# Sixteen more short products of ones ahead of and between the token sums of a transformer block

## The chip, the cores and the metric

The kernel runs on one core of one Trainium2 chip. The metric is the device time of one execution in microseconds (us), from the launch of the program to its end. Engines are named as in the profile: PE is TensorE (matrix products), PEld its weight loads, DVE is VectorE, ACT is ScalarE, POOL is GpSimd, SP is SyncE, which here issues nearly all DMA transfers.

## The reference

The reference is one layer of a diffusion backbone with 256 latent and 256 context tokens of width 2048, in float32. The parts at the start of the layer are the ones that matter here.

```python
mod_lat = jnp.split((jax.nn.silu(c) @ w_mod[layer] + b_mod[layer])[:, None, :], N_MOD, axis=-1)
mod_ctx = jnp.split(jax.nn.silu(c_ctx) @ w_mod[layer] + b_mod[layer], N_MOD, axis=-1)
...
u_lat = modulate(rms_norm(h_lat, norm_mix_w[layer]), mod_lat[0], mod_lat[1])
u_ctx = modulate(rms_norm(h_ctx, norm_mix_w[layer]), mod_ctx[0], mod_ctx[1])
k_na, v_na, k_ret, v_ret, q_na, q_ret, g_ret = jnp.split(u_lat @ w_in[layer], LAT_SPLITS, axis=-1)
```

After that come two kinds of attention, an output projection, a second norm, a router and 16 experts of three 2048 x 1024 matrices each, whose weights are most of the 593 MB that the kernel moves.

## The kernel before

The program is written out by hand, one instruction stream for each engine, with semaphores between them. SP's stream loads the tokens in four pieces of 1 MB (`xnT`, line 485), and then the weights in items of 1 MB (line 514) in one fixed order into a ring of slots. An item ("mod", i, q) holds part q of 4 of the modulation weights for two 128-wide slices, an item ("w", b, q) part q of 4 of block b of the input projection. Eight groups of modulation items (i = 0 to 7) and the items of blocks 0 and 1 come first. SP waits for a slot to be given back before it loads into it a second time.

PE's stream opens so. The norm of each token needs the sum of its squares. ACT squares piece j (line 1069), DVE folds it (lines 1350 and 1351) and says so with `folded`, and PE adds it over the partitions with four products with a column of ones, `token_sums(j)` (line 735). When all four are in, DVE forms the mean (line 1353), POOL the root (line 1826), DVE four diagonal pieces (line 1357), and PE spreads them over the partitions (line 757). `mod_item(i, q)` (line 592) multiplies an item of modulation weights with the two conditioning vectors, 16 products of 32 x 512. `mod_sums(i)` (line 603) adds them up, `project(b, k)` (lines 636 to 638) multiplies a slice of the normed tokens with a slice of `w_in`. `keep_clock(n)` (line 746) is n products of a 128 x 128 tile of ones with itself. They go to a bank whose content is not used, and they wait for nothing but PE itself. The trace has two matmul records for each float32 product.

In this order PE's stream goes on without a choice at run time:

```python
pe.wait_ge(c_act, 2)
mod_item(0, 0)
mod_item(0, 1)
pe.wait_ge(diag_ok, 1)
mm(bank[4][:, :], ones[:, :], diag, start=True, stop=True).then_inc(rstd_pe, 1)
mod_item(0, 2)
mod_item(0, 3)
keep_clock(2)
mod_sums(0)
keep_clock(10)
pair(0)
for i in range(1, MOD_BEFORE - 1):
    mod_item(i, 0)
```

`pair(0)` is project(0, 0) and project(1, 0). After it come the four items of i = 1, and from there a group of modulation items and two steps of the projection by turns. `mod_item` waits for its item's landing (`wait_item`), and `project` for the split of its weights by ACT (line 1093) and DVE (line 1427).

Of the kernel before, what the change touches and what calls it, by code (L numbers as in the profile page):

```python
# [180 lines left out]
def build(nc, x, x_cols, cond, w_mod_a, w_mod_b, b_row, w_in, rpb, w_out,  # L181
# [301 lines left out]
    def _(sp):  # L483
# [49 lines left out]
        for i in ring_items[:RING]:  # L533
            d = moe_pairs[ring_place(i)]
            if i == 2:
                sp.wait_ge(masks, 8)
                sp.dma_start(extra_a[:, :, :].rearrange("p a n -> p (a n)"), w_down[0, EXTRA - 8][:, 0:2048]).then_inc(extra_full, 16)
                sp.wait_ge(roped, ROPED)
                sp.wait_ge(ret_mix_a, 4)
                sp.wait_ge(a_ready, MOD_BEFORE + 1)  # L540
                sp.dma_start(extra_b[:, :, :].rearrange("p a n -> p (a n)"), w_down[0, EXTRA - 8][:, 2048:3584]).then_inc(extra_full, 16)
            if d < 2:
                for s in (2 * d, 2 * d + 1):
                    _, b0, q0 = items[max(n for n in range(n_items) if slot[n] == s)]
                    sp.wait_ge(lo_split, place(b0, 4 * q0 + 3) + 1)
            if d == 4:
                sp.wait_ge(chunk_used, CHUNKS * (NB + NO))
                sp.dma_start(extra_c[:, :], w_down[0, EXTRA - 8][:, 3584:4096]).then_inc(extra_full, 16)
                for s in range(2):
                    sp.dma_start(halves[s][:, :], w_gate[0, SPLIT][:, 2048 * s:2048 * s + 2048]).then_inc(half_full[s], 16)  # L550
            if d == 5:
                sp.wait_ge(r_pe, 1)
            expert_item(0, i, ring_place(i))
# [28 lines left out]
    def _(pe):  # L582
# [148 lines left out]
        def token_sums(j):  # L731

            pe.wait_ge(folded, j + 1)
            for t in range(4):
                last = mm(bank[5][:, t:t + 1], stat[:, j, P * t:P * t + P], ones[:, 0:1], start=j == t == 0, stop=j == 3 and t == 3)
            last.then_inc(token_sq, 1)
# [6 lines left out]
        def keep_clock(n, b=3):  # L743

            for _ in range(n):
                mm(bank[b][:, 0:P], ones[:, :], ones[:, :], start=True, stop=True)

        pe.wait_ge(pool_init, 2)
        keep_clock(18)
        for j in range(4):  # L750
            token_sums(j)
            keep_clock(5 if j < 3 else 1)
        pe.wait_ge(c_act, 2)
        mod_item(0, 0)
        mod_item(0, 1)
# [1224 lines left out]
```

## Time and profile before

| what | value |
|---|---|
| median of 3 runs | 1686.28 us |
| lowest and highest run | 1685.04, 1690.88 us |
| the profiled execution's own time | 1685.8 us |
| its span, first to last instruction | 1683.7 us |
| mean granted TensorE clock | 0.914 |
| PE busy | 1446.7 us (86%) |
| DMA | 593.05 MB, mean 352 GB/s |

The span leaves out 2.1 us around the instructions. How to read them: the work between the launch and the first instruction and behind the last is in the run's time and not in the span. The page cuts the span into 40 equal slices of 42 us. A clock of 1.0 there is 2.4 GHz, one of 0.5 is 1.2 GHz.

### The profile page before, as it was taken

Reading aid. Unit: us, or ns where it says so; the run is one execution under the profiler, and the core shown is the slowest. Engines: PE = TensorE matmul, PEld = TensorE weight load, DVE = VectorE, ACT = ScalarE, POOL = GpSimd, SP = SyncE. Lnnn points to the kernel's source line nnn. Section 1 sums busy time; section 2 is a strip of 40 time slices with the busy share of each in tenths; the row PEclk is TensorE's granted clock in tenths of the full one; section 3 lists DMA queues with packets and bytes.
Section 4 is the critical chain, followed back from the end, with each engine's and each line's share of the span. In section 5 each row is a group of like instructions: output and inputs, shape, how many; then the busy total and the mean of one; then the engine's idle time right before and its main releaser. Section 6 shows DMA issues by size and latency. Waiting matters only on the chain.

```text
span 1683.7 us, 19822 instructions
## 1 busy us (share of the span) xinstructions
PE 1446.7 (86%) x8024; PEld 862.2 (51%) x8024; DVE 713.8 (42%) x1150; ACT 328.0 (19%) x576; POOL 124.3 (7%) x113
## 2 busy tenths in 40 slices
PE   8999999999999999989878687767787677786786
PEld 6678788878888777875212241321332122332232
DVE  4446777678778876662122122112221211421122
ACT  3343333233333345530000000000000000000001
POOL 0000000013322254001000000000000000000002
PEclk8999999999999999999878798787888978977899
DMA  9996658657746767899999999999999999999996
GB/s 398 420 422 233 227 200 300 226 212 254 257 153 247 274 226 156 214 421 427 428 428 427 426 428 429 428 428 427 422 420 428 429 427 428 427 428 428 428 428 281
DMA packets 55980, 593.05 MB, mean 352 GB/s; under 512 B 6348, under 2 KB 6476, under 8 KB 8152
## 3 DMA queue, kind: packets, MB, share of 16 engines
q1 hardware_dynamic: 54584, 585.66, 86.3%
q10 hardware_dynamic: 1312, 6.16, 1.0%
q8 instruction: 66, 1.08, 0.3%
q14 instruction: 18, 0.15, 0.0%
HBM read 588.65 MB, written 2.10 MB: 351 GB/s over the span
## 4 chain that ended last, share of the span: by engine, by line
PE 52%; DMA 41%; DVE 4%; issue 1%; ACT 1%; SPq 0%; POOL 0%; DVEq 0%; POOLq 0%; ACTq 0%
DMA ring<-in_w_up 18%; DMA ring<-in_w_down 17%; PE bank L640 7%; PE bank L642 7%; PE bank L641 7%; PE bank L993 5%; PE bank L927 3%; PE bank L636 3%; PE bank L637 2%; PE bank L638 2%; PE bank L906 2%; PE bank L592 2%; DMA ring<-in_w_gate 2%; PE bank L894 1%; DMA ring<-in_w_down_last 1%
## 5 line engine op out<-in xcount | busy, mean ns | idle before, releaser
L993 PE MATMUL bank<-ring,xg 128*32 128x512 f32 x1504 | 219.6, 713 | 126.9 <-DMA ring<-in_w_up 96.1
L1427 DVE TENSOR_TENSOR whl<-ring,whl 128x512 fp32r<-128x512 f32 x276 | 211.2, 768 | 133.9 <-ACT whl L1093 132.6
L1093 ACT ACTIVATE whl<-ring 128x512 fp32r<-128x512 f32 x276 | 173.1, 629 | 271.0 <-PE bank L642 212.1
L640 PE MATMUL bank<-whl,uh 128*128 128x512 f32 x512 | 206.5, 403 | 2.0 <-DVE tmp L1456 0.7
L642 PE MATMUL bank<-whl,ul 128*128 128x512 f32 x512 | 199.8, 390 | 0.0
L641 PE MATMUL bank<-whl,uh 128*128 128x512 f32 x512 | 199.5, 390 | 0.0
L993 PEld LDWEIGHTS bank<-ring,xg 128*32 128x32 f32 x1504 | 44.9, 120 | 280.1 <-DMA ring<-in_w_up 148.2
L1410 DVE SCALAR_TENSOR_TENSOR part<-ring,csT,part 128x1024 f32<-128x1024 f32 x104 | 140.0, 1346 | 0.1
L1293 ACT ACTIVATE gup<-bank 128x512 f32<-128x512 f32 x32 | 18.7, 597 | 599.0 <-PE bank L993 599.0
L906 PE MATMUL bank<-yy,gcur 128*128 128x512 f32 x252 | 130.3, 642 | 4.7 <-DVE yy L1714 3.5
L1768 DVE COPY gup<-bank 128x512 f32<-128x512 f32 x32 | 22.0, 689 | 247.5 <-PE bank L993 247.4
L1714 DVE TENSOR_TENSOR yy<-bank,m 128x512 f32<-128x512 f32 x64 | 40.0, 684 | 188.5 <-PE bank L927 185.0
L1721 DVE TENSOR_TENSOR acc<-acc,bank 128x512 f32<-128x512 f32 x96 | 65.8, 687 | 125.8 <-PE bank L906 125.8
L640 PEld LDWEIGHTS bank<-whl,uh 128*128 128x128 f32 x512 | 96.2, 188 | 25.9 <-DVE tmp L1456 2.0
L642 PEld LDWEIGHTS bank<-whl,ul 128*128 128x128 f32 x512 | 96.1, 188 | 20.6
L641 PEld LDWEIGHTS bank<-whl,uh 128*128 128x128 f32 x512 | 96.3, 188 | 19.0 <-issue 0.5
L927 PE MATMUL bank<-ring,hT 128*32 128x512 f32 x480 | 67.3, 690 | 34.1 <-DMA ring<-in_w_down 34.1
L906 PEld LDWEIGHTS bank<-yy,gcur 128*128 128x128 f32 x252 | 44.7, 199 | 98.6 <-issue 79.8
L636 PE MATMUL bank<-uh,whl 128*128 128x512 f32 (+1 forms) x256 | 90.7, 354 | 0.7 <-DVE kT L1438 0.4
L637 PE MATMUL bank<-uh,whl 128*128 128x512 f32 (+1 forms) x256 | 86.3, 337 | 0.0
L638 PE MATMUL bank<-ul,whl 128*128 128x512 f32 (+1 forms) x256 | 86.1, 336 | 0.0
L962 PEld LDWEIGHTS bank<-small,gup 128*128 128x128 f32 x512 | 77.2, 241 | 10.3 <-ACT gup L1293 10.3
(263 smaller groups left out, 1623.1 us busy)
## 6 DMA issues: line engine op xcount, KB each, us to landing
ring<-in_w_up SPq DMA_DIRECT2D x61, 2048.0 KB, 26.0
ring<-in_w_gate SPq DMA_DIRECT2D x33, 2048.0 KB, 25.9
ring<-in_w_mod_b SPq DMA_DIRECT2D x63, 1024.0 KB, 5.3
ring<-in_w_down SPq DMA_DIRECT2D x30, 2048.0 KB, 27.0
ring<-in_w_in SPq DMA_DIRECT2D x53, 1024.0 KB, 5.0
ring_b<-in_w_gate SPq DMA_DIRECT2D x15, 2048.0 KB, 21.6
ring_c<-in_w_gate SPq DMA_DIRECT2D x15, 2048.0 KB, 24.1
ring<-in_w_mod_a SPq DMA_DIRECT2D x28, 1024.0 KB, 16.2
```

The lines of the kernel that those rows point to most:

```text
L636: mm(to, wh[:, cols], hi[:, k, 0:n], start=k == 0 and not (shared and t >= 2), stop=False)
L637: mm(to, wl[:, cols], hi[:, k, 0:n], start=False, stop=False)
L638: last = mm(to, wh[:, cols], lo[:, k, 0:n], start=False, stop=k == KC - 1 and not (shared and t < 2))
L640: mm(ps, hi[:, k, cols], wh, start=k == 0, stop=False)
L641: mm(ps, hi[:, k, cols], wl, start=False, stop=False)
L642: last = mm(ps, lo[:, k, cols], wh, start=False, stop=k == KC - 1)
L906: mm(comb_bank(g, ei, cb, t)[:, :], gcur[:, P * t:P * t + P], yy[:, cb, :], start=True, stop=True).then_inc(comb, 1)
L927: last = mm(bank[cb][32 * quad:32 * quad + 32, :], hT[:, r, :], pieces[4 * (r % 2) + cb], start=r < 4, stop=r >= 4)
L993: last = mm(bank[2 * m + half][32 * kk:32 * kk + 32, :], xg[:, 4 * j + kk, CAP * ei:CAP * ei + CAP], parts[kk // of][0][:, kk % of, 512 * ...
L1093: a(whl[:, cidx % (AHEAD + 1), 0, :], slot_buf(slot[n])[:, 512 * (k % 4):512 * (k % 4) + 512], ACT.Copy).then_inc(hi_split, 1)
L1410: ins = v.scalar_tensor_tensor(out=acc, in0=w, scalar=csT[:, k, 0:1], in1=acc, op0=ALU.mult, op1=ALU.add)
L1427: v.tensor_tensor(whl[:, cidx % (AHEAD + 1), 1, :], slot_buf(slot[n])[:, 512 * (k % 4):512 * (k % 4) + 512], whl[:, cidx % (AHEAD + 1), 0, ...
```

## The change

Only the arguments of five calls of `keep_clock` change. There are 25 calls instead of 18 ahead of the first token sum, 12 instead of 5 behind it, 6 instead of 5 behind the second and the third, and 1 as before behind the fourth. That is 16 calls more, or 32 records of the trace.

```diff
         pe.wait_ge(pool_init, 2)
-        keep_clock(18)
+        keep_clock(25)
         for j in range(4):
             token_sums(j)
-            keep_clock(5 if j < 3 else 1)
+            keep_clock((12, 6, 6, 1)[j])
         pe.wait_ge(c_act, 2)
```

PE's instructions at the start of the program, where `ones` is the tile of ones, `stat` the folded squares and x the number of calls in a row:

```order
-L746 MATMUL bank<-ones 128x128 x18
+L746 MATMUL bank<-ones 128x128 x25
 L735 MATMUL bank<-ones,stat 128x1 x4
-L746 MATMUL bank<-ones 128x128 x5
+L746 MATMUL bank<-ones 128x128 x12
 L735 MATMUL bank<-ones,stat 128x1 x4
-L746 MATMUL bank<-ones 128x128 x5
+L746 MATMUL bank<-ones 128x128 x6
 L735 MATMUL bank<-ones,stat 128x1 x4
-L746 MATMUL bank<-ones 128x128 x5
+L746 MATMUL bank<-ones 128x128 x6
```

No instruction has changed its place. PE's stream is longer by the 16 calls, and those of DVE, ACT, POOL and SP are the same.

## Rows read from the trace of the kernel before

**Rows 1.** Page: PE, the clock and the DMA rows of the 40 slices

```profile
PE   8999999999999999989878687767787677786786
...
PEclk8999999999999999999878798787888978977899
DMA  9996658657746767899999999999999999999996
GB/s 398 420 422 233 227 200 300 226 212 254 257 153 247 274 226 156 214 421 427 428 428 427 426 428 429 428 428 427 422 420 428 429 427 428 427 428 428 428 428 281
```

**Rows 2.** Timeline of PE, 1 to 31 us: start, length, line, operation, count, [idle before]

```profile
1.45 6.32 PE L746 MATMUL bank<-ones 128*128 128x128 f32 x36 [1.45 <-POOL mhalf L1823]
9.64 1.05 PE L735 MATMUL bank<-ones,stat 128*128 128x1 f32 x8 [1.87 <-DVE stat L1351]
10.55 1.36 PE L746 MATMUL bank<-ones 128*128 128x128 f32 x10
13.63 1.87 PE L735 MATMUL bank<-ones,stat 128*128 128x1 f32 x8 [1.71 <-DVE stat L1351]
15.36 2.48 PE L746 MATMUL bank<-ones 128*128 128x128 f32 x10
...
23.74 3.13 PE L592 MATMUL bank<-ring,csT 128*32 128x512 f32 x16
26.81 1.12 PE L757 MATMUL bank<-pb,ones 128*128 128x512 f32 x2
27.86 1.92 PE L592 MATMUL bank<-ring,csT 128*32 128x512 f32 x16
```

**Rows 3.** Busy time by stretch: bounds, length, engines (records), granted clock, DMA, GB/s

```profile
7.77:12.58 4.81, 2.27 (x18) 2.08 (x18) 2.74 (x3) 2.56 (x4) 0.00 (x0) 1.00 1.02 429
12.58:16.00 3.42, 2.37 (x11) 2.38 (x12) 2.82 (x4) 2.84 (x2) 0.00 (x0) 0.50 1.00 424
...
22.82:26.23 3.41, 3.41 (x16) 1.29 (x20) 1.03 (x5) 0.00 (x0) 1.02 (x1) 0.50 1.01 420
26.23:34.23 8.00, 7.56 (x59) 4.44 (x51) 4.21 (x11) 3.13 (x6) 0.00 (x0) 1.00 1.02 423
```

**Rows 4.** Timeline of DVE, 12 to 28 us: the folds, the mean, the diagonal

```profile
12.88 0.69 DVE L1351 TENSOR_TENSOR stat<-sq 128x512 f32<-128x512 f32 x1
...
17.85 0.69 DVE L1351 TENSOR_TENSOR stat<-sq 128x512 f32<-128x512 f32 x1
23.21 0.16 DVE L1353 TENSOR_SCALAR rs<-bank 128x4 f32<-128x4 f32 x1 [4.68 <-PE bank L735]
24.67 0.87 DVE L1357 TENSOR_SCALAR pb<-small,rs 128x128 f32<-128x128 f32 x4 [1.29 <-POOL rs L1826]
```

**Rows 5.** Tile `ring` on SP's queue, 4.45 to 4.90: the transfer of item (mod, 0, 3)

```profile
L514 SPq DMA_DIRECT2D ring<-in_w_mod_a x1: 495/495/495, 4.4 to 4.4; - x1
...
DMA to landing us min/median/max: 21.6/21.6/21.6
```

**Rows 6.** The same, 12.55 to 12.60: item (mod, 1, 3), and who waited

```profile
L514 SPq DMA_DIRECT2D ring<-in_w_mod_a x1: 2107/2107/2107, 12.6 to 12.6; - x1
...
  PEld bank L592: 0.5, 1
...
DMA to landing us min/median/max: 28.4/28.4/28.4
```

**Rows 7.** Weight loads of PE at the items of i = 1

```profile
40.35 0.13 PEld L592 LDWEIGHTS bank<-ring_c,csT 128*32 128x32 f32 x4 [0.30 <-issue]
40.97 0.37 PEld L592 LDWEIGHTS bank<-ring,csT 128*32 128x32 f32 x8 [0.49 <-DMA ring<-in_w_mod_a]
```

**Rows 8.** Timeline of PE, 38.5 to 42.5 us: the products of these items

```profile
41.21 1.04 PE L592 MATMUL bank<-ring,csT 128*32 128x512 f32 x8
42.18 0.50 PE L636 MATMUL bank<-uh,whl 128*128 128x512 f32 x1
```

**Rows 9.** Busy time by stretch, columns as before: the stage of modulation, and late ones

```profile
41.21:60.00 18.79, 18.79 (x126) 13.29 (x119) 6.80 (x19) 6.32 (x12) 0.00 (x0) 1.00 1.01 420
60.00:100.00 40.00, 40.00 (x266) 27.62 (x265) 18.79 (x42) 15.38 (x27) 0.00 (x0) 1.00 1.01 420
100.00:130.00 30.00, 30.00 (x198) 21.59 (x197) 15.46 (x33) 13.92 (x24) 0.00 (x0) 1.00 0.99 403
130.00:160.00 30.00, 30.00 (x145) 25.32 (x144) 20.66 (x27) 12.23 (x20) 0.00 (x0) 1.00 0.60 225
...
674.80:678.10 3.30, 3.30 (x13) 2.73 (x12) 3.19 (x5) 2.46 (x6) 0.00 (x0) 0.50 1.00 417
```

## The prediction

> **What bounds the kernel now.** I read the page first. The slices show two regimes [rows 1]: PE at 9 tenths through the first 17 or so slices, and DMA at 9 tenths in the first three and again from slice 18 to the end, at 420 to 429 GB/s. So the first three slices, where the change lies, are full on both sides, and a gain on PE has to be held against the stream of weights there.
>
> Next I read PE's own timeline at the start [rows 2]. The reader is to see two things. The engine has a gap of 1.87 us ahead of the first token sum and one of 1.71 us ahead of the second, with only 10 records of ones between. And the same group of 10 records takes 1.36 us at 10.55 and 2.48 us at 15.36. The granted clock says why [rows 3]: it falls from 1.00 to 0.50 (2.4 to 1.2 GHz) at 12.58, behind a stretch of 4.81 us in which PE was busy for 2.27, and it comes back at 26.23, after the first modulation products. From 13.63 to 26.23 all PE work is at half speed, and PE has no gap in it.
>
> Then I asked who would have held PE there at full speed. DVE's folds end at 12.88 + 0.69 = 13.57 and 17.85 + 0.69 = 18.54 [rows 4], yet DVE starts the mean of all four only at 23.21, after 4.68 us of idling for PE. So PE is the late one there.
>
> Last I asked what PE meets behind that. Item (mod, 0, 3) lands at 4.4 + 21.6 = 26.0 [rows 5], and item (mod, 1, 3) at 12.6 + 28.4 = 41.0 [rows 6]. For the second of these the weight load of PE already idles 0.49 us and starts at 40.97, where the one before it started at 40.35 [rows 7], so the landing is just ahead of 40.97; the products that need it start at 41.21 [rows 8]. PE is kept from a gap only because 0.24 us of earlier products were still in it. **That is the place which decides.**
>
> **The change part by part.** The ones ahead of the first sum: 14 records more. At full speed one costs 1.36 / 10 = 0.136 us by its group of 10. The first 36 took 6.32 us, 0.176 us each, so a part of them ran slower; the added ones come last. 14 x 0.136 = 1.9 us at most, against a gap of 1.87 us whose end DVE sets [rows 2]. Cost 0 to 0.1 us on a sum that is not late.
>
> Behind the first sum: 14 records more, again up to 1.9 us, against 1.71 us of gap [rows 2]. The 24 records start at 10.55 and end by about 13.3 to 13.8 where DVE's fold is there at 13.57. Cost 0 to 0.2 us.
>
> Behind the second and third: 2 records more each, 0.27 us at full speed, 0.5 us at half speed (2.48 / 10 = 0.25 each).
>
> What they are to bring is the full clock through the opening. At full speed a token sum takes 10.55 - 9.64 = 0.91 us and 12 records of ones 12 x 0.136 = 1.6 us, together 2.5 us, which is DVE's own pace (12.88 to 17.85 is two folds, 2.5 us each). So the last sum starts by DVE's last fold, at 18.6, and ends at about 19.6 where it ended at 23.2: **3.6 us earlier**. Two modulation items (16 records) take 1.92 us at 27.86 [rows 2] in place of 3.13, another 1.2 us, so that PE spreads the diagonal at about 22.0 (mean at 19.6, then the same 24.67 + 0.87 - 23.21 = 2.3 us to the diagonal [rows 4]) in place of 26.81. **Up to here 4.8 us are gained.**
>
> Now the stream takes it back. Item (mod, 0, 3) is the second half of the pair at 27.86, used from 27.86 + 0.9 = 28.8 on, and is not there before 26.0: of the 4.8 us, 2.8 are left. By the same steps as before (mod_sums, the new norms, pair(0)) PE comes to the items of i = 1 about 2.8 us earlier. There (mod, 1, 3) is not in before 40.9, and its products can start no earlier than some 0.05 us behind the load at 40.97. They started at 41.21. **0.2 us are left.** Nothing makes the transfer itself earlier: its issue at 12.6 waits for no use of a slot, as it is a first filling, and up to 130 us DMA is 0.99 to 1.02 busy at 403 to 424 GB/s [rows 3, 9], so its queue is never empty. From 41 us on PE has no gap up to 130 and beyond [rows 9], and 0.2 us passes on. At 130 DMA's share falls to 0.60, and later the experts' stream starts on what PE has done, so the 0.2 us should reach the end.
>
> A page of the Trainium skill bears on that limit. DMA: Bandwidth & Descriptors, section Where 436 GB/s comes from, puts the limit of transfers from HBM at about 358 GB/s for a core and that of the fabric at 435. The trace disagrees with the first (420 to 429 GB/s, one core busy) and agrees with the second. Were the opening held to 358 GB/s instead, item (mod, 1, 3) would land some 7 us later and the change would be worth nothing at all; at 435 it would land about 1.2 us sooner, and about 1.4 us of gain would be left.
>
> Sum against the profiled execution: 1685.8 - 0.2 = 1685.6 us. That execution lies 0.5 us under the median of the runs shown. In other executions the clock may come back later than 2.5 us behind the first modulation product (23.74 to 26.23). A spell of half clock that goes on for another 3.3 us, as the one at 674.80 lasts [rows 9], would hold the kernel before up by half of that, 1.65 us, and the changed kernel not. So the gain against the median lies between 0.2 and 1.9 us, and I take the middle, 0.9: **1685.4 us**, or 0.05%. About 0.3% (5.1 us) is what a measurement of this kernel can tell from no change; the three runs shown are 5.8 us apart.
>
> **The rivals.** *The gain passes.* If item (mod, 1, 3) were not a wall (it lands earlier, or its use can be put off by other work), 2.8 us would remain from the first wall, 1683.0, and with none at all 4.8 us, 1681.0. For it speak the 4.68 us for which DVE plainly idles for PE [rows 4]; against it the 0.49 us of idling of the weight load, which is a direct record.
>
> *Slower: the clock falls at the new wall.* PE gets to the items of i = 1 about 2.8 us early. An item of 1.05 MB at 421 GB/s lands every 2.5 us, so (mod, 1, 2) is in at 38.5, where PE asks for it at 41.21 - 0.96 - 2.8 = 37.5 or so, and (mod, 1, 3) at 40.95, where PE is through with the one before it at 39.4 (an item takes 1.92 / 2 = 0.96 us): gaps of 1.0 and 1.6 us within 5 us. In the opening such a pattern, 2.54 us of idling in 4.81, was followed by the low clock [rows 3]. Here a fall would hit work that bounds the kernel from 41 us on. A spell of 3.3 to 3.5 us [rows 9] costs half of itself, 1.7 us: 1685.8 - 0.2 + 1.7 = 1687.3. It decides the sign from a spell of 0.4 us on, and is seen in a measurement only from 10.2 us on. The spell of the opening, 26.23 - 12.58 = 13.65 us, would cost 6.8 us: 1692.4; but there PE had little to do, and here the projections stand ready. The gaps are also shorter than there and the items between them dense.
> The Trainium skill has this as a rule, in TensorE: Matmul & The Clock Gate, section HAM oscillation — how this bites in real kernels: bursts of products that are cut by waits for transfers start cold again and again. By it this rival would be the likeliest, since the change turns a slow but even PE into a fast one that waits for DMA.
>
> *The change doesn't hold the clock.* 12 records between the second, third and fourth sum are only 2 more than in the group that preceded the fall. If the clock falls anyway, at 12.6 or at 16, the opening is as before or slightly better, the wall is the same, and the time is 1685.6 to 1685.8. At half clock the four added records there cost 1.0 us of PE, of which the wall has 0.2 to hide: at worst 1686.5.
>
> **How the numbers follow.** The wall holds and PE stays fast: 0.70. The clock is not held: 0.10. The gain passes: 0.06. The clock falls at the wall: 0.14, with 0.03 of it for a long spell. Over 0.3% faster needs 1681.2 or less: the 4.8 us case of the first rival, and chance in the runs, 0.05. Over 0.3% slower, 1691.3 or more: the long spell and chance, 0.05. Within: 0.90. The range goes from the case of 2.8 us, 1683.0, to the short spell with 1.2 us on top for the scatter of the runs, 1688.5.
>
> **What the profile should show.** Right: PE's row of ones at 1.45 has 50 records and ends near 9.4, the granted clock is 1.00 to past 30, DVE's L1353 starts near 19.6 in place of 23.21, L757 near 22 in place of 26.81. Then PE idles for DMA ahead of L592, for about 3 us in all before 41, and the products of (mod, 1, 3) start at 41.0. Wrong: they start clearly earlier than 40.9 (the stream isn't the wall), or a stretch behind 36 us has a clock of 0.50 (the rival on the slow side), or L1353 starts near 23 (the clock wasn't held). A difference of over 3 us with these products still at 41.0 would mean that something behind 130 us moved, for which I have no mechanism.

## The result, and the profile after

| kernel | median | runs | lowest, highest |
|---|---|---|---|
| before | 1685.36 us | 22 | 1683.61, 1690.88 |
| changed | 1689.26 us | 22 | 1685.16, 1692.33 |

The ratio is 1.0020, with a 95% interval of 1.0013 to 1.0026. The change makes the kernel 3.9 us slower. The prediction was 1685.4 us, 0.05% faster, with a range that ends at 1688.5. It was wrong in sign and range. The difference is under the 0.3% that the text took for the limit of a measurement, but over 22 runs on each side it stands clear of none. The profiled execution took 1689.32 us, with a span of 1687.5.

The page of the changed kernel, its first line and the DMA rows of the slices that answer to [rows 1]:

```profile
span 1687.5 us, 19886 instructions
...
PEclk9999999999999999999988788887788877977899
DMA  9996658657646757799999999999999999999997
GB/s 396 421 421 233 225 200 302 224 216 254 251 160 241 289 208 169 197 425 427 427 428 428 428 427 427 428 428 428 413 395 427 428 428 428 428 428 428 428 427 294
```

There are 64 instructions more than the 19822 of the kernel before: each of the 16 calls is two weight loads and two products. The first slice's clock is at 9 tenths in place of 8. And slices 28 and 29 (counted from 0, 1181 to 1266 us) have 413 and 395 GB/s, where the kernel before has 422 and 420 at nearly the same place and no number below 420 between there and the last slice.

The opening, PE's timeline of the changed kernel (columns as in [rows 2]):

```profile
1.45 7.63 PE L746 MATMUL bank<-ones 128*128 128x128 f32 x50 [1.45 <-POOL mhalf L1823]
9.87 1.05 PE L735 MATMUL bank<-ones,stat 128*128 128x1 f32 x8 [0.79 <-DVE stat L1351]
...
22.29 1.13 PE L757 MATMUL bank<-pb,ones 128*128 128x512 f32 x2
23.61 1.06 PE L592 MATMUL bank<-ring,csT 128*32 128x512 f32 x8 [0.20 <-DMA ring<-in_w_mod_a]
26.09 1.07 PE L592 MATMUL bank<-ring,csT 128*32 128x512 f32 x8 [1.42 <-DMA ring<-in_w_mod_a]
```

and at the items of i = 1, where the kernel before stood as in [rows 8]:

```profile
38.53 1.06 PE L592 MATMUL bank<-ring_c,csT 128*32 128x512 f32 x8 [0.61 <-DMA ring_c<-in_w_mod_a]
41.01 1.06 PE L592 MATMUL bank<-ring,csT 128*32 128x512 f32 x8 [1.42 <-DMA ring<-in_w_mod_a]
42.01 0.50 PE L636 MATMUL bank<-uh,whl 128*128 128x512 f32 x1
```

This is what was forecast. The diagonal is spread at 22.29 in place of 26.81, 4.5 us earlier. Then PE waits for three transfers, and the products of (mod, 1, 3) start at 41.01 in place of 41.21: 0.2 us are left. In this execution no stretch of the opening has a low clock, neither behind the first sum, where the kernel before had 0.50, nor at the new waits:

```profile
12.58:16.00 3.42, 3.28 (x30) 3.09 (x29) 2.81 (x4) 2.85 (x2) 0.00 (x0) 1.00 1.00 422
...
37.00:41.21 4.21, 2.19 (x24) 0.33 (x19) 0.24 (x1) 0.00 (x0) 0.00 (x0) 1.00 1.01 416
41.21:44.60 3.39, 3.39 (x19) 2.18 (x12) 0.00 (x0) 1.12 (x2) 0.00 (x0) 1.00 1.02 425
```

So the 3.9 us are lost elsewhere. The slices point at the experts' stage, and shorter stretches within them at 1215 to 1230 us. PE's timeline of the kernel before there:

```profile
1200.60 5.80 PE L906 MATMUL bank<-yy,gcur 128*128 128x512 f32 x12 [0.33 <-DVE acc L1721]
1211.85 5.49 PE L894 MATMUL bank<-ohr,h 128*128 x24 [5.46 <-issue]
1217.27 2.00 PE L993 MATMUL bank<-ring,xg 128*32 128x512 f32 x16
```

and of the changed kernel:

```profile
1203.09 5.80 PE L906 MATMUL bank<-yy,gcur 128*128 128x512 f32 x12 [0.33 <-DVE acc L1721]
1214.02 1.86 PE L894 MATMUL bank<-ohr,h 128*128 x7 [5.13 <-issue]
1219.33 4.00 PE L894 MATMUL bank<-ohr,h 128*128 x17 [3.46 <-issue]
1223.26 2.15 PE L993 MATMUL bank<-ring,xg 128*32 128x512 f32 x16
```

Line 906 is the last work of an expert group, line 894 the first of the next (the gather of its tokens). Groups 1 and 2 share one piece of code, a loop of PE that is passed twice, so between these two lines PE jumps back to the loop's start. Both kernels idle there for over 5 us, and the releaser is "issue": no semaphore, no data. The changed kernel does 7 of 24 products and idles another 3.46 us. From the end of line 906 to the start of line 993 it takes 14.4 us in place of 10.9.

The kernel before has the same change of groups twice more, without a jump: into group 1, and out of the loop into group 3. There the gather follows with no idle time, or with 0.78 us of waiting for DVE:

```profile
973.33 3.04 PE L894 MATMUL bank<-ohr,h 128*128 x24
1446.19 3.14 PE L894 MATMUL bank<-ohr,h 128*128 128x128 f32 x24 [0.78 <-DVE acc L1721]
```

What that does to the stream, busy time by stretch (columns as in [rows 3]), before:

```profile
1150.00:1215.00 65.00, 46.85 (x237) 17.28 (x235) 14.79 (x24) 2.86 (x4) 0.00 (x0) 0.81 1.01 428
1215.00:1230.00 15.00, 14.10 (x111) 8.44 (x114) 5.51 (x16) 0.00 (x0) 0.00 (x0) 0.92 0.96 391
```

and after:

```profile
1150.00:1215.00 65.00, 46.79 (x242) 15.39 (x235) 14.39 (x23) 2.86 (x4) 0.00 (x0) 0.83 1.01 427
1215.00:1230.00 15.00, 11.54 (x76) 7.76 (x75) 3.64 (x10) 0.00 (x0) 0.00 (x0) 0.71 0.77 304
```

In 15 us the changed kernel moves (391 - 304) x 15 = 1.3 MB less. At 428 GB/s these are 3.0 us. Behind that the stream runs at 427 to 429 GB/s in all slices but the last, in both kernels, so it has little to catch up with. That the hole reaches the end of the kernel is argued from this; the run with the waits behind the loop, below, shows that it need not do so in full.

### The profile page after: what moved, and what is told of

Same layout as the page of the kernel before. It is cut to its first block and busy times, and to the rows that moved or that the text cites. A ratio compares the mean times of both kernels' runs of the same rounds, so it can differ in the third digit from the quotient of the medians.

```text
span 1687.5 us, 19886 instructions
## 1 busy us (share of the span) xinstructions
PE 1451.0 (86%) x8056; PEld 862.3 (51%) x8056; DVE 714.3 (42%) x1150; ACT 328.1 (19%) x576; POOL 125.7 (7%) x113
## 5 line engine op out<-in xcount | busy, mean ns | idle before, releaser
L993 PE MATMUL bank<-ring,xg 128*32 128x512 f32 x1504 | 226.5, 733 | 123.3 <-DMA ring<-in_w_up 93.7
L906 PE MATMUL bank<-yy,gcur 128*128 128x512 f32 x252 | 128.7, 635 | 5.2 <-DVE yy L1714 3.5
L906 PEld LDWEIGHTS bank<-yy,gcur 128*128 128x128 f32 x252 | 44.1, 197 | 98.7 <-issue 80.7
L927 PE MATMUL bank<-ring,hT 128*32 128x512 f32 x480 | 63.7, 658 | 31.9 <-DMA ring<-in_w_down 31.9
```

The costliest lines, as they stand in the source:

```text
L906: mm(comb_bank(g, ei, cb, t)[:, :], gcur[:, P * t:P * t + P], yy[:, cb, :], start=True, stop=True).then_inc(comb, 1)
L993: last = mm(bank[2 * m + half][32 * kk:32 * kk + 32, :], xg[:, 4 * j + kk, CAP * ei:CAP * ei + CAP], parts[kk // of][0][:, kk % of, 512 * ...
```

## The experiments

Three theories were set against each other. **A, the place of the code:** the 64 instructions push the rest of PE's code along, and the jump back lands where the code that is fetched first runs out after a few instructions. **B, the opening:** the early work or the clock does the harm. **C:** scatter of the clock late in the kernel.

The expectations give the kernel before as 1685.4 us. In the runs that went with the first four experiments it had 1685.46 (29 runs), with the last two 1685.66 (21 runs).

### The same shift without the products

```diff
+        for _ in range(24):
+            pe.wait_ge(pool_init, 1)
         pe.wait_ge(pool_init, 2)
         keep_clock(18)
+
+        def idle_waits(n):
+
+            for _ in range(n):
+                pe.wait_ge(pool_init, 2)
+
         for j in range(4):
+            if j == 0:
+                idle_waits(52)
+            if j == 1:
+                idle_waits(52)
             token_sums(j)
             keep_clock(5 if j < 3 else 1)
```

`idle_waits(n)` is n waits for a semaphore that is long up. Two of them become one instruction (the page of the profile counts 19886, again 64 more than 19822), so that these are 26 and 26 instructions, and the 24 waits at the start are 12.

> The kernel before, with 64 instructions that only wait for a semaphore that is already up, put where PE idles anyway in the opening (12 at the start, 26 ahead of the first token sum, 26 ahead of the second). They move the rest of PE's code as far as the 16 added calls do (64 instructions: 32 weight loads and 32 products), but warm nothing. Theory A (code place: PE's jump back in its loop at 1205 us lands so that the code behind the jump runs out after 7 products, and a second fetch is waited for): a second idle time of some 3 us behind the jump, as in the changed kernel (3.46 us), the transfers' rate falls there, and the time is 3 to 4 us over the kernel before: 1688.5 to 1689.5. Theory B (the opening: the early items or the clock do the harm): the opening is as before, one idle time at the jump, 1685.4 +- 0.8. Theory C (scatter of the clock late in the kernel): no difference beyond 1 us.

Measured: 1688.72 us (12 runs), ratio 1.0018 (1.0009 to 1.0026). PE at the jump back; the edit moves line numbers by 12, so that L906 here is the gather:

```profile
1211.97 1.86 PE L906 MATMUL bank<-ohr,h 128*128 x7 [5.51 <-issue]
1217.56 3.92 PE L906 MATMUL bank<-ohr,h 128*128 x17 [3.73 <-issue]
```

and the stream behind it:

```profile
1220.00:1225.00 5.00, 5.00 (x39) 3.42 (x38) 1.89 (x6) 0.00 (x0) 0.00 (x0) 0.87 0.53 157
```

The second idle time is there, behind the same seventh product, though the opening is the old one (its first group of ones still has 36 records, from 2.61 us on in place of 1.45). The hole in the stream is there too. Theory A holds; B and C can't give this.

### The same instructions behind the loop

```diff
+        for _ in range(128):
+            pe.wait_ge(pool_init, 2)
         pe.wait_ge(comb_add, 3 * 32 + 1)
         for ei in range(4):
             expert(3, ei, down_columns if ei == 3 else down_rows)
```

> The same 64 waiting instructions, put behind PE's loop, ahead of the last group of four experts. The loop's code keeps its place. Theory A: as the kernel before, 1685.4 +- 0.8, and one idle time of 5.5 us at the jump. If added instructions as such cost (fetching them, issuing them), it is slower by as much as the kernel with them ahead. Theory B: as before, too.

Measured: 1686.18 us (11 runs), ratio 1.0004 (0.9995 to 1.0013). At the jump:

```profile
1211.97 4.34 PE L894 MATMUL bank<-ohr,h 128*128 x24 [5.48 <-issue]
```

One idle time, and no difference in the whole that can be told from none.

But the 64 waits are not free where they stand. They hold PE between groups 2 and 3, where it had idled for 0.78 us:

```profile
1451.71 5.46 PE L894 MATMUL bank<-ohr,h 128*128 128x128 f32 x24 [6.14 <-issue]
```

That is about 0.1 us for each (the 12 at the start of the run before put the first ones off by 1.16 us, 0.1 us each as well), and the products behind them run slower (5.46 us for the 24 in place of 3.14). The stream has a hole there too: 393 GB/s over 1440 to 1480 us, where the kernel before has 427, which is 3.2 us of stream. Yet the time is only 0.7 us longer, and the interval ends at 2.2. So this run shows two things. With the loop's code in its old place there is no second idle time at the jump. And a hole of some 3 us in the stream need not cost 3 us; what becomes of it at this place was not found.

### Four and eight calls more

```diff
         keep_clock(2)
         mod_sums(0)
-        keep_clock(10)
+        keep_clock(14)
         pair(0)
```

This on the changed kernel, and the same with 18.

> The changed kernel with 4 more products of ones ahead of the first projection, where it has 2.6 us to spare by its trace (16 instructions more, 80 over the kernel before). Theory A: in the changed kernel the code behind the jump runs out after about 17 instructions; 16 more bring that down to about 1, so there is still a second idle time, of 5 to 6 us now in place of 3.46: 1690 to 1692, and no less than 1689. Theories B and C: 1689.3, as the changed kernel.

> The changed kernel with 8 more products of ones ahead of the first projection (32 instructions more, 96 over the kernel before). Theory A: the boundary of the fetched blocks now lies ahead of the jump's target, so one block of 256 instructions serves nearly whole behind the jump, and there is one idle time only: 1685 +- 0.8, some 4 us faster than the changed kernel, although it does more work. Theories B and C: 1689.3 or more, as the changed kernel.

Measured: with four 1693.11 us (5 runs), ratio 1.0036 (1.0022 to 1.0050); with eight 1686.82 us (12 runs), ratio 1.0007 (0.9998 to 1.0016). PE at the jump with four more:

```profile
1200.93 9.49 PE L906 MATMUL bank<-yy,gcur 128*128 128x512 f32 x16 [0.88 <-DVE yy L1714]
1221.65 4.57 PE L894 MATMUL bank<-ohr,h 128*128 x24 [11.24 <-issue]
```

its stream behind it, slower than that of any other run here:

```profile
1220.00:1225.00 5.00, 3.35 (x15) 3.35 (x16) 0.73 (x2) 0.00 (x0) 0.00 (x0) 0.50 0.40 167
1225.00:1230.00 5.00, 4.99 (x43) 3.32 (x41) 2.18 (x6) 0.00 (x0) 0.00 (x0) 0.99 0.21 46
```

and with eight more:

```profile
1214.22 4.36 PE L894 MATMUL bank<-ohr,h 128*128 x24 [5.17 <-issue]
```

This is the strongest of the runs, since the effect is not monotonic. The changed kernel gets through about 17 instructions behind the jump before it idles again (7 pairs of weight load and product, and a few on registers). With 16 instructions more in front, it gets through none that the trace shows: both idle times merge to 11.24 us, and the time is 1693.1, 1 us over the upper end that was expected. With 32 more the second one is gone and the kernel is 2.4 us faster than the changed one, with more work. The time expected, 1685 +- 0.8, was missed by 1 us.

### The loop written out

```diff
-        with pe.Fori(1, 3) as g:
+        for g in (1, 2):

             pe.wait_ge(y_ok, g * 16 + 1)
```

> The kernel before with PE's loop over expert groups 1 and 2 written out, so that PE makes no jump back. Nothing else changes. Theory A (the jump back makes PE wait for code, 5.46 us idle in the kernel before): that idle time is gone. The transfers' rate there was 383 to 406 GB/s in place of 426 for 15 us, so some 1 us at most was lost by it, and the time is 0 to 1 us under the kernel before: 1684.4 to 1685.5. If the longer code of PE costs fetches that matter, it is slower than 1685.5.

> The changed kernel with the same loop written out. Theory A: the place of the code no longer matters, so its 3.9 us over the kernel before are gone, and it is within 1 us of the other kernel with the loop written out. What is left between these two is the worth of the opening alone: -0.2 us by my sum for an execution like the profiled one, up to -1.9. Theory B' (the early opening itself also costs something, since the changed kernel and its two variants got their first w_out item 1.5 to 3.7 us late at 674 us, and the three kernels with the old opening did not): this kernel is 1 to 2 us slower than the other, and PE is again 2 us late behind 674.

Measured: on the kernel before 1685.30 us (11 runs), ratio 0.9998 (0.9989 to 1.0007); on the changed one 1685.53 us (11 runs), ratio 0.9999 (0.9990 to 1.0008). At the place of the old jump, in the kernel before with the loop written out:

```profile
1200.57 5.89 PE L906 MATMUL bank<-yy,gcur 128*128 128x512 f32 x12 [0.49 <-DVE acc L1721]
1206.30 3.04 PE L894 MATMUL bank<-ohr,h 128*128 128x128 f32 x24
1209.27 1.92 PE L993 MATMUL bank<-ring,xg 128*32 128x512 f32 x16
```

and in the changed one:

```profile
1200.91 5.90 PE L906 MATMUL bank<-yy,gcur 128*128 128x512 f32 x12 [0.49 <-DVE acc L1721]
1206.64 3.04 PE L894 MATMUL bank<-ohr,h 128*128 128x128 f32 x24
```

No idle time in either, and all 3.9 us are gone. What stands between these two kernels is the opening alone: 0.2 us the wrong way, far inside both intervals. So the opening that the change makes is worth nothing that can be measured. The cost of 1 to 2 us that theory B' expected isn't there either. Writing the loop out doesn't beat the kernel before either: its one idle time of 5.46 us was nearly covered by what the ring of experts' weights still had free (391 in place of 428 GB/s for 15 us, 1.3 us at most), and 0.1 to 0.4 us is all that the medians show.

All runs side by side. The second column is PE's idle time by "issue" at the jump. The fourth turns the third into time: what the stream moved less than in the kernel before from 1200 to 1240 us, at 428 GB/s. The last is the median against that of the kernel before, measured along with it.

| kernel | idle at the jump, us | GB/s, 1200 to 1240 us | stream lost, us | time, us |
|---|---|---|---|---|
| before | 5.46 | 414 | 0 | 0 |
| changed | 5.13 + 3.46 | 378 | 3.4 | +3.9 |
| before, waits ahead | 5.51 + 3.73 | 374 | 3.7 | +3.3 |
| before, waits behind | 5.48 | 416 | -0.2 | +0.7 |
| changed, four more | 11.24 | 333 | 7.6 | +7.6 |
| changed, eight more | 5.17 | 422 | -0.7 | +1.4 |
| before, written out | none | 428 | -1.3 | -0.4 |
| changed, written out | none | 429 | -1.4 | -0.1 |

The three kernels with a second or a merged idle time lose about what their stream loses there, and the others nothing that is clear of the noise.

One thing stays open. In all four kernels with the new opening the first item of `w_out` was late, by ACT's wait for it. The row of the kernel before, and that of the changed kernel:

```profile
672.84 1.15 ACT L1093 ACTIVATE whl<-ring 128x512 fp32r<-128x512 f32 x2 [4.88 <-DMA ring<-in_w_out]
```

```profile
674.56 1.15 ACT L1093 ACTIVATE whl<-ring 128x512 fp32r<-128x512 f32 x2 [6.75 <-DMA ring<-in_w_out]
```

The other three with the new opening have 674.3, 674.3 and 676.5, the other three with the old one 672.3, 672.7 and 673.0. In the changed kernel with the loop written out, most of its 1.5 us is there from 45 us on (see the clock, below). For the other three it was not found how an opening that is 0.2 us earlier at 41 us gives 1.5 us or more at 674. PE's work is not behind in the changed kernel, SP issues the item at 651.15 us in place of 651.32, and it lands 23.4 us later in place of 21.5, through a stretch (654 to 668 us) in which DMA is 0.9 busy and moves only 27 to 30 GB/s in both kernels. In time it comes to little: the medians of the two kernels with the loop written out differ by 0.2 us, those of eight calls more and of waits behind the loop by 0.6, which their intervals don't tell from nothing.

## Why the prediction was wrong

**The clock in the opening: right.** The granted clock stayed at 1.00 behind the first sum in all four kernels with the new opening. The mean of the sums of squares started at 19.91, where 19.6 was forecast and 23.21 was the old start, and the diagonal was spread at 22.29 for a forecast of 22.0.

**The wall at item (mod, 1, 3): right.** 41.01 for a forecast of 41.0. The waits for DMA ahead of it were 0.20, 1.42, 0.61 and 1.42 us, 3.65 in all against "about 3". The weight load that idled 0.49 us for the transfer [rows 7] was the row that gave this away.

**The gain in other executions: not seen.** I added 0.7 us for executions in which the clock comes back later. The two kernels with the loop written out show no such gain. (The middle between 0.2 and 1.9 us is 1.05, not 0.9; nothing hangs on it.)

**The clock falling at the wall: not in the changed kernel's trace, but in one of the four with the new opening.** The changed kernel has 1.00 from 37.00 us on, in spite of gaps of 0.61 and 1.42 us. The changed kernel with the loop written out, behind gaps of 0.60 and 1.52 us, has this (a row of PE's timeline, and a stretch with columns as in [rows 3]):

```profile
40.96 1.94 PE L592 MATMUL bank<-ring,csT 128*32 128x512 f32 x8 [1.52 <-DMA ring<-in_w_mod_a]
...
40.96:44.60 3.64, 3.64 (x13) 1.66 (x14) 0.00 (x0) 1.11 (x2) 0.00 (x0) 0.53 1.02 425
```

These eight products take 1.94 us in place of 1.06, and PE comes to the next `mod_sums` (line 603) at 46.42 in place of 44.86, 1.6 us behind. That is the second rival with the size it was given, 1.7 us. It got a chance of 0.14. One execution of four can't tell how often it happens, and in the medians it doesn't show, but it can take away more than the 0.2 us that the opening gives.

**What failed is the cost of the added products.** I priced them as work ("cost 0 to 0.1 us on a sum that is not late") and as nothing else, and wrote that the 0.2 us "should reach the end". Their 64 instructions also move everything that PE runs after them, 1200 us later included. The step that was left out is: which jumps does this engine make, what does it wait for there now, and does the change move the target? The term put at nothing is a second wait at PE's loop jump, 3.46 us of idling that leaves a hole of 3.0 us in a saturated stream; in time it is 3.3 us by the waits ahead and 3.9 us by the change. The prediction's last sign, a difference of over 3 us with the products of (mod, 1, 3) still at 41.0, is what came: it said that then something behind 130 us had moved, and had no mechanism for it. The trace of before had the row for it: 5.46 us of idle time by "issue" in the middle of the experts' stage. The prediction rests on rows of the first 160 us and one at 674.80, and for the rest on slices.

**What the wait is for.** The page of the profile lists a kind of DMA of its own, the fetches of instructions:

```profile
q8 instruction: 67, 1.10, 0.3%
```

That is 16 KB each. The kernel before has 66. The count alone says little, since the kernel with the waits behind the loop has 67 too; it matters when the fetches go out. While PE idles at the jump, one goes out among the weights. In the changed kernel a second one goes out in the second idle time; here is the view of the DMA queues from 1213.8 to 1219.3 us (packets, MB, share), and from 1215.9 on it is the same one:

```profile
q1 hardware_dynamic: 160, 2.33, 99.8%
q8 instruction: 1, 0.02, 1.2%
```

Taken in stretches of 0.1 us, the second fetch goes out 5.7 to 6.1 us behind the first in all six kernels that jump, whether PE runs dry or not: at 1209.1 and 1215.1 us in the kernel before, at 1211.2 and 1216.9 in the changed one. So what the place of the code decides is whether the instructions of the first fetch last PE until the second has landed.

Runtime: NRT & Kernel Launch of the Trainium skill, section Instruction fetch mechanics, says that an engine's code is brought in blocks of 16 KiB, 256 instructions, one behind the other, and that a taken branch to code that is not held makes the engine wait for the target's block. The traces agree with it: 16 KB a fetch, and in the kernel before with the loop written out 16048 weight loads and products of PE to 63 fetches, 255 to each.

The block of 256 instructions explains the swing of the experiments: with 64 added, a boundary lies some 17 instructions behind the target, with 80 about 1, with 96 it lies ahead of it and the whole next block serves. By the same count it lies about 81 behind with none added, and PE is still busy with these when the second fetch goes out at 1215.1 (it has no gap from 1211.85 on). That the wait is for code is inferred from "issue", from the times of these fetches and from the way it answers to shifts; no record names it.

## What to carry to other kernels

Instructions that "cost nothing" still take a place in the engine's code, and a loop behind them may pay. Before adding or removing some, look for idle time by "issue" behind a loop's jump, count how many instructions the engine gets through there, and ask what a saturated stream has in reserve: here 5.5 us of idling cost some 0.4 us by the medians, and 8.6 us and more cost 3.3 to 7.6. When two versions differ by a fraction of a per cent, measure them with the loop written out, or with the code shifted by a few dozen idle instructions, before believing the difference.

And before speeding up an engine's first work, look for the first transfer that it waits for behind that. If a weight load idles for it already, the gain ends there, however large it was, and the new waits can cost the clock.

## What was new about the hardware

The wait for code at this jump was long, with the DMA queues full of weights: 5.13 to 5.51 us in the five kernels that have it apart from the merged one, and 11.24 us for the merged one, of two blocks. The fetch's own packet takes only some 1.1 us of that. The blocks are fetched one after the other there, 5.7 to 6.1 us apart, not together. No run has the jump with the queues empty, so what of this is due to the weights stays open.

Going through straight code costs nothing like it: the kernels with the loop written out have no idle time at this place.

The clock falls in such an idle time. The stretches of the kernel with four more calls show it, at 0.50 with no product running:

```profile
1215.00:1220.00 5.00, 0.00 (x0) 0.00 (x0) 0.00 (x0) 0.00 (x0) 0.00 (x0) 0.50 0.92 390
```

so the products behind the jump run slow for a while as well: the 24 of line 894 take 4.34 to 5.49 us behind one idle time, and 3.04 us where there is none.

And the same waits for DMA in the opening, gaps of 0.6 and 1.4 to 1.5 us, left the clock at 1.00 in one execution and were followed by 3.3 us at half clock in another.
